# Second mixer of a two-layer block on one Trainium2 core: ScalarE evicts the sixth turned tile ahead of the first split of the weight columns, and those columns are loaded ahead of four modulation slices

## What the reference computes

```python
x_lat = x_lat + mod_lat[5] * y[n_ctx:].reshape(B, S, D)      # end of the first layer's experts
...
h_lat = modulate(rmsnorm(x_lat, g_mix[l]), mod_lat[0], mod_lat[1])
h_ctx = modulate(rmsnorm(x_ctx, g_mix[l]), mod_ctx[0], mod_ctx[1])
...
u = h @ w_in                                                 # w_in is 1024 x 4096
xm, z = u[..., :MLSTM_E], u[..., MLSTM_E:]
```

## Time and profile before

| | us |
|---|---|
| median of 3 runs | 2460.28 |
| lowest and highest of them | 2458.04, 2461.36 |
| the profiled execution, its own time | 2461.31 |
| span of the profile, first to last instruction | 2459.7 |

### The profile page before, as it was taken

The page is one execution under the profiler, slowest core; times in us unless marked ns, Lnnn a source line. Parts: engine busy times, 40 slices in busy tenths (PEclk is TensorE's granted clock), DMA queues, the critical chain, the costliest instruction groups (busy, mean ns, idle before and its releaser), DMA issues.

```text
span 2459.7 us, 42712 instructions
## 1 busy us (share of the span) xinstructions
PE 2321.2 (94%) x16387; PEld 1553.2 (63%) x16388; DVE 1625.6 (66%) x2005; ACT 946.8 (38%) x1167; POOL 427.6 (17%) x461
## 2 busy tenths in 40 slices
PE   6999989999999999999969999999999899999984
PEld 3555534457888888888847887666644455555542
DVE  2899985447898889888976651677534633454544
ACT  3000014115777777777754232466421111111111
POOL 0633431220000000000020000211000223233323
PEclk8999989999999999999989999999999899999997
DMA  9111075539999999999992132212543979999997
GB/s 342 58 44 59 34 293 167 182 113 402 421 401 388 380 395 383 385 389 392 378 380 81 62 124 104 87 54 75 193 154 140 412 313 376 404 421 420 420 420 309
DMA packets 154320, 649.12 MB, mean 264 GB/s; under 512 B 27866, under 2 KB 42874, under 8 KB 99458
## 3 DMA queue, kind: packets, MB, share of 16 engines
q1 hardware_dynamic: 126624, 577.40, 59.7%
q0 software_dynamic: 16192, 57.53, 6.5%
q10 hardware_dynamic: 11426, 13.12, 1.5%
HBM read 595.13 MB, written 52.86 MB: 263 GB/s over the span
## 4 chain that ended last, share of the span: by engine, by line
PE 81%; DMA 9%; DVE 4%; ACT 2%; issue 2%; POOL 1%; SPq 0%; ACTq 0%; DVEq 0%; POOLq 0%
PE ps L970 78%; DMA arena<-in_w_dram 6%; DMA chunk<-in_w_ada_dram 1%; ACT arena L1616 1%; DVE arena L2380 1%; PE ps L1212 1%; PE ps L1190 1%; PE ps L1196 1%; DMA arena<-h_d,uix 1%; PE ps L1059 1%; POOL arena L769 0%; DMA buf_d<-arena 0%; PE ps L1586 0%; DMA arena<-in_w_ada_dram 0%; DMA arena<-buf_d,slots 0%
## 5 line engine op out<-in xcount | busy, mean ns | idle before, releaser
L970 PE MATMUL ps<-arena 128*32 128x256 f32 (+5 forms) x10296 | 1188.7, 407 | 38.9 <-DVE arena L2380 12.3
L970 PEld LDWEIGHTS ps<-arena 128*32 128x32 f32 (+1 forms) x10296 | 652.5, 129 | 521.1 <-issue 318.5
L2433 DVE TENSOR_TENSOR wl<-wx,wh 128x2048 fp32r<-128x2048 f32 x228 | 511.1, 2285 | 18.5 <-ACT wh L1616 18.5
L1616 ACT ACTIVATE arena<-ps 128x256 f32<-128x256 f32 (+5 forms) x389 | 176.4, 478 | 864.0 <-PE ps L970 616.9
L1616 ACT ACTIVATE wh<-wx 128x2048 fp32r<-128x2048 f32 x228 | 432.4, 1915 | 80.8 <-PE ps L970 75.9
L2380 DVE COPY arena<-arena 128x2048 f32<-128x2048 f32 x180 | 222.7, 1297 | 273.1 <-PE ps L970 228.8
L970 PE MATMUL ps<-wh,xT 128*128 128x512 f32 x1184 | 379.2, 394 | 1.2 <-issue 0.7
L970 PEld LDWEIGHTS ps<-wh,xT 128*128 128x128 f32 x1184 | 222.5, 188 | 53.1 <-issue 1.2
L2502 DVE SCALAR_TENSOR_TENSOR arena<-arena,par 128x768 f32<-128x768 f32 x232 | 241.1, 1112 | 0.0
L970 PE MATMUL ps<-wl,xT 128*128 128x512 f32 x608 | 239.4, 394 | 0.0
L970 PE MATMUL ps<-wh,gT 128*128 128x512 f32 x608 | 199.5, 399 | 0.0
(11 more groups left out here) (362 smaller groups left out, 2267.1 us busy)
## 6 DMA issues: line engine op xcount, KB each, us to landing
wx<-in_w_dram SPq DMA_DIRECT2D x228, 1024.0 KB, 8.4
arena<-in_w_dram SPq DMA_DIRECT2D x192, 1024.0 KB, 21.8
arena<-in_w_ada_dram SPq DMA_DIRECT2D x40, 1024.0 KB, 8.6
craw<-in_w_in_c_dram SPq DMA_DIRECT2D x8, 2048.0 KB, 8.7
buf_d<-arena POOLq DMA_DIRECT2D x1, 14848.0 KB, 57.5
arena<-buf_d POOLq DMA_DIRECT2D x19, 512.0 KB, 10.0
buf_d<-arena POOLq DMA_DIRECT2D x19, 512.0 KB, 7.7
arena<-in_w_in_ab_dram SPq DMA_DIRECT2D x8, 1024.0 KB, 12.6
```

Source lines behind the costliest of these rows:

```text
L970: return pe.matmul(bank_ap, lhsT, rhs, start=first, stop=last)
L1616: return act.activation(out_, in_, f, **kw)
L2433: v.tensor_tensor(wl[:, g], wx[:, g], whs[g % NH].bitcast(F32), ALU.subtract).then_inc(m["low"], 1)
```

## The change

On SP the load of the first 512 columns moves from the third tile's turn to the first, ahead of the two waits in front of the slices 24 to 27 and so ahead of those slices. On ACT the copy of the sixth turned tile moves ahead of the wait for that load, of the making of `cw0h` and of `vector_out(6)`.

```diff
                     if n == 2 and i == 0:
+                        sp.dma_start(craw, wc[:, :, 0:512]).then_inc(cw, 16)
                         sp.wait_ge(x_new, j + 1 - NT)
                         sp.wait_ge(u_mm, 21)
                         for k in range(24, 28):
                             item_load(k)
-                    if n == 2 and i == 2:
-                        sp.dma_start(craw, wc[:, :, 0:512]).then_inc(cw, 16)
...
                 if n == 2:
+                    turned(n, t, j)
                     act.wait_ge(cw, 16)
                     go(cw0h, craw[:, :, 0:P], ACT.Copy).then_inc(c_high, 1)
                     vector_out(6)
-                    turned(n, t, j)
```

## The result

The changed kernel took 2463.3 us in the median of 22 runs (2461.13 to 2467.75), the kernel before 2460.66 in 22 runs on the same chip (2457.03 to 2463.57). The ratio is 1.0013, with an interval of 1.0007 to 1.0018: 2.6 us more, slower, but by less than the 0.2% named ahead. The forecast was 2463.1. The number was met; the sum behind it was not, and most of what follows is on that. The profiled execution took 2462.91 us with a span of 2461.3, against 2461.31 and 2459.7 before.

A forecast was written before the change was run, and what follows sets the result against it. The chain was taken as PE for 81%, the change's worth lying between experts and second mixer. 2.08 for `cw0h`/`cw0l` plus 0.7 for the fetch gave 2.8 more than the 2460.28 median: 2463.1 us, range 2460.2 to 2465.6.

The forecast's parts named there:

- The pair: `cw0h` and `cw0l`, now behind the sixth copy, delay DVE's first modulated block by 2.08 us; bounds 0 to 2.28.
- The load: Early `craw` load shares the DMA engines with the experts' row fetches, costing the chain 0.7 us; bounds 0 to 5.2.
- the equal split: q0 and q1, both full, share DMA equally; a fetch takes 2.6 us instead of 1.3, chain loses 0.8.
- both readings: Equal shares for both queues, 0.8 us lost, or packets taking turns, `craw` getting a third, 0.3 us lost.
- estimate of one turn: One turn of `craw` ahead of a fetch: 17 times 2 KB on 16 engines, 0.56 MB or up to 1.4 us.
- fetch starved: Rival: q1 served first, tile 0's fetch waits for all of `craw`, 5.2 us; 2467.6 in all; chance 0.07.
- the loss on the second fetch: Fetch 1 lands at 1271.65, so DVE's add of tile 1 starts at 1271.75 against 1270.96: 0.8 us.
- tile 1's add about 0.7 us later: Sign expected in the profile after: DVE's add of tile 1, at 1270.96 before, comes about 0.7 us later.
- Slices late: Rival: slice 27 comes 5.2 us later, delaying PE's 72 matmuls 1.85 us; 4.6 in all, 2464.9; chance 0.13.
- The stores: Stores ACT awaits before the first `hTh` now queue behind the 2 MB load, needed by about 1302.6; cost nothing.
- No price: Rival: fetches finish before `craw` moves and the 2.1 us come back further on; 2460.3; chance 0.10.

The follow-up runs named there:

- behind: Changed kernel with the load of `craw` moved behind SP's two waits, still ahead of the four slices: 2463.27 us, ratio 1.0009 to the kernel before.
- turn_late_load: Kernel with PE turning tile 5 ahead of the 72 small matmuls, load at its old place behind the third tile: 2459.47 us, ratio 0.9990 to before.
- load_only: Kernel before plus the early load of `craw` alone, ACT's order as before: 2462.91 us, ratio 1.0011 to before.
- dve_first: Changed kernel with DVE making the first modulated block ahead of `cw0l`: 2463.21 us, ratio 1.0010 to the kernel before.
- act_only: Kernel before plus ACT's new order alone, load where it was: 2462.79 us, ratio 1.0005 to before.
- turn_first: PE turns tile 5 ahead of the small matmuls, `cw0h` before the sixth copy, vector behind `hTh`, load behind SP's waits: 2457.59 us, ratio 0.9987 to before.

## Why the prediction was right in its number and not in its sum

**The pair (2.08): right, mechanism and size.** Copy to `hTy` went from 1.14 to 3.14, by `cw0h` and `cw0l` as worked out, and taking `cw0l` out of the way on DVE returns all of it to the stage, though not visibly to the time.

**The load (0.7): mis-sized, it is 2.0.** The step that failed is "I take 0.7, near the equal split, because that is what the row with both queues full shows". It was within the bounds, 0 to 5.2, but two things were wrong in it. First, the split is not one of bytes. The DMA queues of the changed kernel from 1266.71 to 1267.71, with packets, MB and share of the engines:

```profile
q0 software_dynamic: 65, 0.27, 67.8%
q1 hardware_dynamic: 67, 0.14, 35.9%
```

As many packets from each, and since those of the fetch are 4 KB and those of `craw` 2 KB, the fetch gets two thirds. In the earlier trace rows both queues moved some 4 KB a packet, so equal packets looked like equal bytes; the forecast had both readings and chose the other. The Trainium skill, DMA: Bandwidth & Descriptors, section "Queues, rings and completion order", has an engine take turns a packet of some 9 to 17 descriptors at a time. Equal counts agree with turns of equal number; how long a turn is can't be read here.

By that alone the fetch would have lost less than 0.7, not more. The second thing makes up for it and had no term at all: the fetch began late. The same view from 1263.71 to 1264.71, 3 us behind the fetch's issue:

```profile
q1 hardware_dynamic: 181, 0.39, 103.4%
```

There is no row of q0. SP's timeline has the issue of `craw` 0.24 us ahead of the fetch's:

```profile
1260.47 0.37 SPq L529 DMA_DIRECT2D craw<-in_w_in_c_dram  x1
```

So `craw` has the engines to itself, while before, at the same distance from the issue, the fetches were under way (the earlier trace rows begin 2.1 us behind it, with 85.1% for the fetches). POOL's instruction for the fetch of tile 0, before and in the changed kernel:

```profile
1261.87 0.97 POOL L928 DMA_INDIRECT arena<-buf_d,slots  x1 [7.24 <-ACT ss L1616]
```

```profile
1260.71 2.00 POOL L927 DMA_INDIRECT arena<-buf_d,slots  x1 [7.20 <-ACT ss L1615]
```

It ends at 1262.84 and 1262.71, and the first packet of q0 moves at 1264.06 and 1266.06: 1.22 us behind the end before, 3.35 now. In all five profiles with the early load this is 3.25 to 3.35 us, in the seven without it 0.69 to 1.22, although earlier loads filled q1 when the fetch was issued there too (99.8% from 1261.87 to 1262.37 before). From its first packet to its landing the fetch takes 2.8 to 3.4 us with the load and 2.7 to 4.3 without. So no loss shows in the split, and the late start accounts for the 2.0. The forecast's estimate of one turn, up to 1.4 us, is too short for it, and why the start is late by this much is not shown. The rival "fetch starved" had the right kind of cause, for 2 us and not for all 2 MB; by its own text it decides from 2.8 us on, and that was not reached.

Two more things in the working were not as read. It put the loss on the second fetch, ahead of tile 1's add, but this add starts 2.46 us behind tile 0's before and 2.47 now, so only the first fetch counts. And its sign for the fetch, "tile 1's add about 0.7 us later", looks nearly met at 1271.50 against 1270.96; but the fetch was issued 1.16 us sooner in the second profile, and from its issue the add is 1.70 us later.

**Slices late: right that they are not, and the delay was about as forecast.** Slice 27 in the changed kernel, its issue in SP's timeline and its KB and us to landing (answers to the earlier trace rows):

```profile
1273.05 0.47 SPq L467 DMA_DIRECT2D arena<-in_w_ada_dram  x1
```

```profile
arena<-in_w_ada_dram SPq DMA_DIRECT2D x1, 1024.0 KB, 16.1
```

It landed at 1273.05 + 16.1 = 1289.15, before at 1289.35. That looks like no delay, but the stages begin 1.16 us apart. From the issue of tile 0's fetch it is 27.5 us before and 28.4 now; in the further profiles 25.1 and 25.7 before, 28.4 and 29.0 in the changed kernel. So the slices come 2.5 us later in the mean, and the forecast had 2.1. They stay hidden since PE comes later too: it arrives 2.6 to 3.4 us behind slice 27 in the changed kernel (2.7 to 4.0 before), more than the 1.3 of the forecast. From 1268.40 to 1272.40 the DMA engines, at a share of 0.32 in the earlier trace rows, are now full:

```profile
1268.40:1272.40 4.00, 2.89 (x48) 1.02 (x40) 3.33 (x3) 0.79 (x1) 2.92 (x2) 0.93 1.04 397
```

How much of `craw` the idle time took up was not tested by itself; `behind`, whose load misses the first part of this stretch, has the late slices.

**The stores: right.** POOL's memset, released by them at 1299.88 in the earlier trace rows, is now released by PE at 1299.47. `turn_late_load` shows what they cost without that cover.

**No price: wrong in the stage, and not wholly wrong in the time.** The stage has 4.5 us more, the median only 2.6 to 2.9 (2463.3 less 2460.66, 2463.56 less 2460.71). 4.5 us would be a ratio of 1.0018, at the edge of the first interval and within the second. The last column of the table leans the same way: from the 512 matmuls to the end the changed kernel is shorter in all three profiles, by 1.7 us from middle to middle. But the profiles scatter by 4.8 us there; `load_only` (1018.19) and `dve_first` (1018.55), which also ask early, are not shorter, and `act_only`, which does not, is the shortest of all (1016.42). The first 426.6 to 426.8 us of that stretch are the same in all kernels but `turn_late_load` (425.9); what differs comes behind them. I found no wait that explains it. Nor is the time shorter where one of the two costs is taken away: 2463.21 in `dve_first`, 2463.27 in `behind`, 2463.3 in the changed kernel. The intervals of 11 runs are some 0.09%, or 2.2 us, wide to each side, so a difference of 2 us can be missed. Whether some 2 us are given back there, or the stage's mean of three profiles is above that of the timed runs, **stays open**. The forecast's 2.8 met the time although its stage was 1.7 us too small (1.3 of it on the fetch), because the time shows less than the stage. That the two differences nearly cancel is luck.

**The small matmuls** had no term in the sum, and two profiles alone would have given them one that is too large. Windows of the kernel before around its 72 (1292.01 to 1296.65), with the granted clock as the third number from the end:

```profile
1288.00:1292.00 4.00, 2.21 (x14) 1.63 (x16) 0.38 (x4) 3.67 (x6) 0.00 (x0) 0.50 1.04 407
1292.00:1294.00 2.00, 2.00 (x29) 0.77 (x32) 0.00 (x0) 1.64 (x2) 0.00 (x0) 0.67 1.05 405
1294.00:1296.60 2.60, 2.60 (x53) 0.97 (x41) 0.00 (x0) 0.66 (x1) 0.00 (x0) 1.00 1.03 404
```

and of the changed kernel around its own (1292.53 to 1298.39):

```profile
1292.50:1294.50 2.00, 2.00 (x21) 0.66 (x24) 0.00 (x0) 1.66 (x2) 0.00 (x0) 0.50 0.06 25
1294.50:1296.50 2.00, 2.00 (x28) 0.73 (x24) 0.00 (x0) 0.00 (x0) 0.00 (x0) 0.56 0.00 0
1296.50:1298.30 1.80, 1.80 (x36) 0.66 (x28) 0.00 (x0) 0.00 (x0) 0.00 (x0) 1.00 0.00 0
```

PE is busy throughout in both and has been since tile 4's turning; the clock goes from 0.50 (1.2 GHz) to 1.00 (2.4 GHz) among the matmuls, and in the changed kernel later. The table says how much of this is the change: 5.08 in the mean of three before, with one of 5.66, and 5.72 after. `load_only` and `dve_first`, with the early load too, have 5.31 and 5.10. Some 0.6 us may be left to the change; three profiles of each can't settle it.

## What to carry to other kernels

Before moving work out of the way of a copy, see what the copy waits for: here PE had not turned the tile, so the work that stood ahead of it was free, and moved behind it, it cost its full length; moving PE's turning (`turn_first`) is what made the copy sooner, and that is faster than both kernels. Read the times of two profiles from a common event, here the issue of tile 0's fetch: on the spans' own clocks the later slices looked as early as before. A load that is asked for early into idle DMA time is not free if a short transfer on the chain is issued just behind it in another queue. And profile each of two close kernels more than once before a difference of 1 us in a stage is called an effect.

## What was not expected of the hardware

A fetch by POOL that was issued 0.24 us behind a 2 MB load in another queue moved its first packet 3.25 to 3.35 us behind the end of POOL's instruction in five profiles, against 0.69 to 1.22 us in seven without that load. Once both queues move, they move equal numbers of packets and not of bytes: 65 and 67 in 1 us, at 4 KB and 2 KB, 67.8% and 35.9%. And the same 72 matmuls took 4.65, 4.92 and 5.66 us in three executions of one program, by when the granted clock rose from 0.50 to 1.00.
